# Four outputs of the next projection from un-normed sums behind four layer norms, and small VectorE steps moved in front

## The reference

```python
def layer_norm(x, g, b):
    mu = jnp.mean(x, axis=-1, keepdims=True)
    xc = x - mu
    var = jnp.mean(xc * xc, axis=-1, keepdims=True)
    return xc * lax.rsqrt(var + LN_EPS) * g + b

def swiglu(x, w_in, w_out):
    gate, up = jnp.split(x @ w_in, 2, axis=-1)
    return (jax.nn.silu(gate) * up) @ w_out
# x = LN0(a*x + swiglu(x)); x = LN1(a*x + rglru_block(x)); x = LN2(a*x + swiglu(x))
# k, v = split(x @ kv_w);   x = LN3(a*x + swiglu(x))
# x = LN4(a*x + dilated_attention(x, k, v, w_q, w_o)); x = LN5(a*x + swiglu(x))
```

## Time and profile before

| what | value |
|---|---|
| median of 3 runs | 1860.36 us (1859.71, 1860.36, 1870.26) |
| the profiled execution | 1870.4 us, its span 1868.6 us |
| TensorE busy | 98% of the span |
| VectorE, ScalarE, GpSimd busy | 68%, 62%, 22% |
| mean granted TensorE clock | 0.991 |

### The profile page before, as it was taken

How to read it: one execution, slowest core, us unless ns; L and a number is a source line. 1 busy time by engine, 2 the same in 40 slices (tenths; PEclk the granted TensorE clock), 3 DMA queues, 4 the chain that set the end, 5 groups by cost and what they waited for, 6 DMA issues and landing times.

```text
span 1868.6 us, 32954 instructions
## 1 busy us (share of the span) xinstructions
PE 1827.5 (98%) x11306; PEld 1608.9 (86%) x11306; DVE 1268.5 (68%) x1916; ACT 1165.7 (62%) x1905; POOL 418.8 (22%) x448
## 2 busy tenths in 40 slices
PE   9999999999999999999999999999999999999998
PEld 8778888898698888888889988889888888788887
DVE  7887776764776766666667866666666565667665
ACT  5476565643655746588548778744687454758853
POOL 4003320230533302021122032211021120632112
PEclk9999999999999999999999999999999999999999
DMA  7525366576353565565635546654656546026662
GB/s 247 173 69 169 114 202 191 182 194 184 108 169 102 192 189 186 177 193 189 216 116 172 186 133 194 204 179 147 187 185 203 201 130 198 35 91 201 184 220 70
DMA packets 87340, 312.11 MB, mean 167 GB/s; under 512 B 10432, under 2 KB 15680, under 8 KB 86976
## 3 DMA queue, kind: packets, MB, share of 16 engines
q1 hardware_dynamic: 86944, 309.01, 53.1%
q10 hardware_dynamic: 288, 1.64, 0.3%
HBM read 309.56 MB, written 1.05 MB: 166 GB/s over the span
## 4 chain that ended last, share of the span: by engine, by line
PE 88%; DVE 5%; ACT 3%; issue 2%; POOL 2%; DMA 0%; SPq 0%; POOLq 0%; ACTq 0%; DVEq 0%
PE pt L520 42%; PE pt L521 21%; PE pt L514 5%; PE pt L515 4%; PE pt L516 4%; PE pt L636 1%; DVE w_lo L1919 1%; PE pt L640 1%; PE pt L638 1%; PE pt L1178 1%; PE pt L959 1%; ACT w_hi L1289 1%; PE pt L1081 0%; POOL spare L2757 0%; PE pt L677 0%
## 5 line engine op out<-in xcount | busy, mean ns | idle before, releaser
L1919 DVE TENSOR_TENSOR w_lo<-raw,w_hi 128x1024 fp32r<-128x1024 f32 (+2 forms) x546 | 705.4, 1293 | 279.3 <-ACT w_hi L1289 271.2
L1289 ACT ACTIVATE w_hi<-raw 128x1024 fp32r<-128x1024 f32 (+2 forms) x546 | 597.6, 1096 | 384.3 <-PE pt L521 223.6
L520 PE MATMUL pt<-in_both,w_hi 128*128 128x512 f32 x2103 | 743.3, 398 | 0.6 <-DVE in_both L2550 0.5
L521 PE MATMUL pt<-in_both,w_lo 128*128 128x256 f32 x2103 | 590.4, 281 | 0.0
L520 PEld LDWEIGHTS pt<-in_both,w_hi 128*128 128x128 f32 x2103 | 395.6, 188 | 98.6 <-DVE w_lo L1919 1.4
L520 PE MATMUL pt<-act_both,w_hi 128*128 128x512 f32 x1309 | 463.9, 399 | 0.0
L521 PEld LDWEIGHTS pt<-in_both,w_lo 128*128 128x128 f32 x2103 | 397.8, 189 | 0.1
L521 PE MATMUL pt<-act_both,w_lo 128*128 128x256 f32 x1309 | 366.7, 280 | 0.0
L520 PEld LDWEIGHTS pt<-act_both,w_hi 128*128 128x128 f32 x1309 | 245.7, 188 | 60.8 <-issue 1.5
L521 PEld LDWEIGHTS pt<-act_both,w_lo 128*128 128x128 f32 x1309 | 247.1, 189 | 0.2
L2722 POOL TENSOR_TENSOR act_both<-scr,act_both 128x256 f32 x88 | 100.3, 1139 | 498.4 <-ACT act_both L1806 498.4
(11 more groups left out here) (341 smaller groups left out, 2337.9 us busy)
## 6 DMA issues: line engine op xcount, KB each, us to landing
raw<-in_fi SPq DMA_DIRECT2D x176, 512.0 KB, 3.6
raw<-in_ff SPq DMA_DIRECT2D x128, 512.0 KB, 3.6
raw<-in_fo SPq DMA_DIRECT2D x64, 704.0 KB, 4.1
raw<-in_dq SPq DMA_DIRECT2D x24, 512.0 KB, 3.7
raw<-in_mq SPq DMA_DIRECT2D x16, 512.0 KB, 4.0
raw<-in_mo SPq DMA_DIRECT2D x16, 512.0 KB, 3.9
raw<-in_rg_u SPq DMA_DIRECT2D x10, 512.0 KB, 3.7
raw<-in_rg_y SPq DMA_DIRECT2D x10, 512.0 KB, 3.6
```

The costliest lines, as they stand in the source:

```text
L520: nc.tensor.matmul(pt[:, b, :], lhs_hi, both.rearrange("p t s -> p (t s)"), start=start, stop=False)
L521: return nc.tensor.matmul(pt[:, b, 0:S], lhs_lo, both[:, 0, :], start=False, stop=stop)
L1289: nc.scalar.activation(w_hi[:, u.slot(), w], raw[:, u.slot(), w], ACT.Copy).then_inc(hi_split, 1)
L1919: v.tensor_tensor(w_lo[:, u.slot(), w], raw[:, u.slot(), w], w_hi[:, u.slot(), w].bitcast(F32), ALU.subtract).then_inc(lo_split, 1)
```

## The change

In front, `gains_scaled`, `softplus_begun`, `softplus_series` and `decays` move from behind `mem_k` to between the first splits of `mem_k`'s units.

Behind norms 1 to 4 (`Z_NORMS`) the next projection's first four outputs no longer wait for the norm. They are computed from z = g*y, the sums before the norm, with two more columns, the gain and the bias themselves. With W the unit's weights, the normed output is rstd * (W z - mean * W g) + W b; the last two columns of each output, W g and W b, are copied to `z_cols`. Three of the outputs run abreast and the fourth behind them, all by `three` with 258 columns. VectorE then does per output `z_open` (mean * column - output, which frees the bank) and `z_scale` (times rstd). The sums over the features become three matmuls with a full 128x128 matrix of ones (256 columns, fp32) between the second and third chunk, so mean and variance come out already spread; the root, the reciprocal (L2701, now on 128x256) and GpSimd's subtraction (all eight chunks) work on full tiles. The residual's eight ScalarE instructions move behind the splits of the next three units. Norms 0 and 5 stay as they were (`plain_norm`).

```diff
+            def from_normed_sums(name, n):
+                z = z_both(n)
+                pe.wait_ge(acc_free, LN_ACC[n] + DC - 1)
+                for k in range(DC):
+                    pe.wait_ge(z_ready, DC * (n - 1) + k + 1)
+                    for j in range(Z_OPEN):
...
+                        mm = three(o, w_hi[:, u % RING, w], w_lo[:, u % RING, w], z[:, k, 0, :], z[:, k, 1, :],
+                                   k == 0, k == DC - 1)
...
+                    if k == 1:
+                        pe.wait_ge(rest_part, REST0[n] + 3)
+                        nc.tensor.matmul(pt[:, 6, 0:S], ones, rest_sum, start=True, stop=True).then_inc(rest_ready, 1)
+                        pe.wait_ge(sq_sum, 6 * (n + 1))
+                        nc.tensor.matmul(pt[:, 4, 0:S], ones, spare[:, 0, :], start=True, stop=False)
+                        pe.wait_ge(lnsq_ready, DC * (n + 1))
+                        nc.tensor.matmul(pt[:, 4, 0:S], ones, spare[:, DC - 1, :], start=False, stop=True
+                                         ).then_inc(var_ready, 1)
+                for j in range(Z_OPEN, Z_WIDE):
...
 # ScalarE
+            def layer_norm(n):
+                z_high(n, DC - 1)
+                act.wait_ge(rest_ready, n + 1)
+                nc.scalar.activation(spread_wide, pt[:, 6, 0:S], ACT.Square, scale=1.0 / D).then_inc(rest_squared, 1)
+                nc.scalar.activation(mean_wide, pt[:, 6, 0:S], ACT.Copy, scale=1.0 / D).then_inc(rest_copied, 1)
+                act.wait_ge(var_done, n + 1)
+                nc.scalar.activation(spread_wide, spread_wide, ACT.Sqrt, bias=lneps).then_inc(ln_root, 1)
+                for k in range(DC):
+                    act.wait_ge(ln_scaled, DC * n + k + 1)
+                    shift(n, in_hi, k).then_inc(in_hi_ready, 1)
+                    if k == 5:
+                        split(Pos(LN_LAST[n] + 1 + RING))
...
 # VectorE
+            def layer_norm(n, name, first):
+                split(Pos(LN_LAST[n] + RING))
+                dve.wait_ge(var_ready, n + 1)
+                dve.wait_ge(rest_squared, n)
+                v.scalar_tensor_tensor(out=spread_wide, in0=pt[:, 4, 0:S], scalar=1.0 / D, in1=spread_wide, ...)
+                z_low(n, DC - 1)
+                dve.wait_ge(ln_root, n + 1)
+                v.reciprocal(rstd_all, spread_wide).then_inc(ln_inverse, 1)
+                for k in range(DC + 2):
+                    if k < DC:
+                        scaled(n, k)
+                    if k == DC - 1:
+                        split(Pos(LN_LAST[n] + 1 + RING))
+                        z_columns(name, 0, Z_OPEN)
+                        z_open(name, 0, first)
...
 # GpSimd
+                    for k in range(DC):
+                        pool.wait_ge(z_ready, DC * (n - 1) + k + 1)
+                        g_.tensor_tensor(y[:, k, :], y[:, k, :], mean_wide, ALU.subtract).then_inc(recentred, 1)
...
 # VectorE, in front
+            split(Pos(2))
+            gains_scaled()
+            softplus_begun()
+            split(Pos(3))
+            softplus_series((17, 15, 13, 11))
```

More of the change, by code:

```diff
@@ L121 @@
 NA_OUT_BANK = (7, 2)
+Z_SCALED0 = starts([("fi01", 2), ("kv_k", 1), ("dq", 1), ("fi11", 2)])
 LN_ACC = [ACC0[name] for name in ("fo00", "rg_out", "fo01", "fo10", "do", "fo11")]
+PLAIN = {0: 0, 5: 1}
+REST0 = [0, 2, 5, 8, 11, 14]
+RECENTRED0 = [0] + [DC - DVE_RECENTRE + DC * n for n in range(5)]
+LN_LAST = [UNIT0[name] + UNITS[name] - 1 for name in ("fo00", "rg_out", "fo01", "fo10", "do", "fo11")]
 PCOL = starts(PARAMS := [
@@ L1786, in swiglu @@
+                if held is not None:
+                    residual(n)
             def swiglu(l, f, n):
@@ L1884, in _ @@
             units("rg_out", after=ln_squares(1), hold=True)
-            layer_norm(1, UNIT0["rg_out"] + 7 + RING)
+            layer_norm(1)
             swiglu(0, 1, 2)
-            units("kv_k")
+            for j in range(1, 4):
+                split(Pos(UNIT0["kv_k"] + j + RING))
+            residual(2)
+            units("kv_k", begun=4)
             units("kv_v")
             swiglu(1, 0, 3)
-            act.wait_ge(ln_root, 4)
+            for j in range(1, Z_WIDE):
+                split(Pos(UNIT0["dq"] + j + RING))
+            act.wait_ge(z_scaled, Z_SCALED0["fi11"])
             act.dma_start(chunks(spare, 0, 8)[:, 0:3 * TRI], dram["dist"]).then_inc(dist_landed, 16)
@@ L2174, in _ @@
                 mem_low(Pos(k))
-            for u in range(2, RING):
-                split(Pos(u))
             def gains_scaled():
@@ L2540, in layer_norm @@
                 link(e)
[L2541 removed]
+                dve.wait_ge(rstd_wide, PLAIN[n] + 1)
                 for k in range(DC + 2):
@@ L2552, in layer_norm @@
                                                op0=ALU.add, op1=ALU.subtract).then_inc(in_ready, 1)
-                split(Pos(held))
+                if held is not None:
+                    split(Pos(held))
             def swiglu(l, f, n):
@@ L2651, in _ @@
             lru_lo(RC // 2 - 1)
-            units("rg_out", before=into_y_centred(1), hold=True)
-            layer_norm(1, UNIT0["rg_out"] + 7 + RING)
+            units("rg_out", before=into_y_centred(1), hold=True, ahead=z_ahead(1))
+            layer_norm(1, "fi01", act_b[0])
             swiglu(0, 1, 2)
```

296 lines of the change are left out of this document (235 added, 61 removed).

## The result

The changed kernel takes 1881.88 us (median of 4 runs, 1879.19 to 1883.01); the kernel before, run beside it, 1863.19. The ratio is 1.0087, interval 1.0067 to 1.0108: **slower by 0.9%**, some 16 us; the two medians lie 18.7 us apart. A gain of 1.5 us was forecast. The profiled execution has a span of 1877.4 us, 8.8 more than that of before.

The account below looks back on a forecast made before the run. TensorE, busy 98% of the span, bounds the kernel; 4.2 us gained in front less 2.7 lost at the norms (29.2 against 26.5) gives 1.5 us less, set against the 1860.36 median: 1859 us, range 1843 to 1871.

Parts of the forecast that it names:

- In front: Small VectorE steps moved ahead: TensorE starts in_t at 62.0 in place of 64.20, no clock fall; gain 4.2 us, range 0.5 to 5.
- The rival in which nothing comes in front: Later mem_k carries through and the clock falls anyway, so 4.2 us becomes 0.5: 1863 us; chance 0.1.
- Output 4: Fourth output behind each of norms 1 to 4 waits 2.4 us for VectorE, slowed beside GpSimd; lower bound 0.5.
- the slower rival: GpSimd's subtractions behind norms held back to 1.7 us each: 1870 us; two clock falls at unit 8 look alike, 1863; chance 0.2.
- Unit 8 of `fi01` and `fi11`: Behind norms 1 and 4 TensorE waits 3.2 us for unit 8's split, with ScalarE's residual ahead of it.
- 258 columns, the three sums: TensorE's added matmul work: three fp32 sums, 1.3 us per norm; 258 columns run as 256, under 0.1 us per norm.
- Between the last output and the sums: TensorE waits 1.6 us ahead of the sums at norms 2 and 3 only, 0.6 if GpSimd's addition does not slow.
- Behind `kv_k` and in `dq`: Behind norm 2 kv_v waits 1.8 us for VectorE's splits and key writing; behind norm 3 dq waits nothing.
- The clock: TensorE's clock falls behind waits cost 2 us each; left out of the sum and kept in the range.
- its signs of being wrong: Matmuls of 258 columns slower than 0.12 us, subtractions over 1 us, or no wait at unit 8.
- The first rival: VectorE's chain behind the norms keeps up, residual finds idle time: norms 14 us against 26.5, 16.7 less in all, 1844; chance 0.25.

Follow-up runs that it names:

- e4: Changed kernel with the reciprocal behind norms 1 to 4 written to a PSUM bank in place of SBUF; 1875.42 us, ratio 1.0041 to the kernel before.
- e6: Changed kernel with 16 unused matmuls on TensorE ahead of the wait for output 4 behind norms 1 to 4; 1882.36 us, ratio 1.0096 to the kernel before.
- e1_residual: Changed kernel with ScalarE's residual moved behind fi01 and fi11 (norms 1, 4) and ahead of the wait for dq's queries (norm 3); 1869.24 us, ratio 1.001.
- e3: Changed kernel with VectorE writing the last chunk of y ahead of three low parts of z; 1871.36 us, ratio 1.0028 to the kernel before.
- e7: Changed kernel with residual moved, last y ahead of low parts of z, and reciprocal in PSUM, all together; 1853.77 us, ratio 0.9925 to the kernel before.
- e2: Changed kernel with unit 4 split earlier on ScalarE and VectorE and output 0 opened earlier behind norms 1 to 4; 1883.44 us, ratio 1.0097.
- e8: Changed kernel with the edits of e7 plus the earlier split and opening of e2; 1857.43 us, ratio 0.9942 to the kernel before.
- f2: The kernel of e7 run once more, on the chip of the changed kernel; 1854.52 us, ratio 0.9938 to the kernel before.

## Why the prediction was wrong

It had the sum of the waits right, in part by luck, and the sign of the whole wrong. Step by step:

- **In front.** Forecast: start at 62.0, no fall, 4.2 gained. Measured: 61.88, 1.00 at 64 to 66, and -4.30 by the ninth chunk. It then lost 1.6 at 82 to 87, where the clock fell in this profile though TensorE was never idle; this happened in three of the eleven profiles with this front (this one, e4 and e6). The step held. The rival in which nothing comes in front did not.
- **Output 4.** Forecast 2.4 everywhere, by VectorE slowed beside GpSimd. Measured 2.65, 2.45, 2.65, 1.59, and e4_psum showed the reason to be the one given. GpSimd at 0.82 was in the range of the earlier trace rows; the slower rival, 1.7 us a subtraction, did not happen.
- **Unit 8 of `fi01` and `fi11`.** Forecast 3.2, by the residual. Measured 3.42 and 3.43, and e1_residual removed them.
- **258 columns, the three sums.** As counted. Products of 258 columns start 0.36 us apart as those of 256, and their matmuls are as long (296, 286 and 283 ns in the grouped view, against 288, 283 and 283). The three sums hold TensorE from 1084.18 to 1085.39, 1.2 us, where 1.3 was counted.
- **Between the last output and the sums.** Forecast a first wait at norms 2 and 3 only, 1.6 us. Measured 1.25 there, and 0.94 and 2.48 at norms 1 and 4: `y` stands behind three low parts of z on VectorE, and GpSimd's addition takes 1.57 beside the split. That I saw for norms 2 and 3 and not for 1 and 4 was a miss of 3.4 us. About half of it was made good by the first waits at norms 2 and 3, 0.7 us shorter together than forecast, and by smaller waits at units 5 to 7, 1.1 us.
- **Behind `kv_k` and in `dq`.** I had the chains the wrong way round: 1.8 for `kv_v` and nothing for `dq`. Measured: nothing (hidden behind the slow clock, 1.1 without it) and 1.80, since ScalarE, waiting for the queries of VectorE, did the residual late. The two errors, each of 1.8 us, cancel; that is luck.
- **The clock.** This is **the step that failed**: "A fall costs half of the four us behind it, 2 us each; I leave it out of the sum and in the range." The price was about right and the count was not: the term that the sum put at nothing measured 8 to 11 us over the four norms (the table below), and that alone turns the gain of 1.5 us into a loss. I argued from one idle time of two us that left the clock up and one of 4.42 that did not, and had just worked out six waits of 2.4 to 3.2 us. Five falls came, behind waits of 3.42, 2.45, 2.65, 2.48 and 3.43. The prediction did name two falls at unit 8, at 4 us, in its slower rival, but kept them out of the forecast, and its signs of being wrong have no clock in them. Nor was the idle time of two us a safe ground. It is the one ahead of norm 4, 2.17 us in the kernel before and 2.17 to 2.19 in all twelve profiles, and in three of them (e1, e3, e7) a fall followed. This is e1:

```profile
1651.78 1.22 PE L1162 MATMUL pt<-scr,con 128*128 128x256 f32 x2 [2.18 <-POOL scr L3034]
```

```profile
1652.00:1654.00 2.00, 2.00 (x8) 1.82 (x9) 0.96 (x3) 0.51 (x2) 0.00 (x0) 0.50 0.85 317
```

The price of each norm, waits and all, beside the forecast. The measured total is the excess before plus the shift by position. The matmuls are as counted in the prediction. What waits and matmuls leave of the total is put down to the falls.

| norm | before | forecast | measured | of it waits | matmuls | left | falls |
|---|---|---|---|---|---|---|---|
| 1 | 5.7 | 8.2 | 11.5 | 7.55 | 1.5 | 2.4 | 1 |
| 2 | 7.4 | 7.1 | 7.0 | 3.70 | 1.3 | 2.0 | 1 |
| 3 | 7.4 | 5.5 | 9.8 | 5.70 | 1.5 | 2.6 | 1 |
| 4 | 6.0 | 8.2 | 13.6 | 8.04 | 1.5 | 4.1 | 2 |
| sum | 26.5 | 29.0 | 41.9 | 25.0 | 5.8 | 11.1 | 5 |

Waits were 25.0 where 23.2 were forecast. By this subtraction the falls are 11.1 of the 12.9 us by which the norms are dearer than forecast, 2.2 us each; by the one fall that was there in the first profile and missing in the second, 1.6 each, they would be 8. Either way they are most of the miss at the norms. The first rival, in which VectorE keeps up and the residual finds idle time, forecast 14 us for the four norms and 1844; e7_three is that case, made: 26.5 - 9 = 17 us for the norms. It is 13.5 us under the kernel before, where the rival had 16.7.

Three things more had a part in the distance to the median. A fall in front and one in the attention, which the kernel before did not have in its profile, cost 1.6 us each. The range, 1843 to 1871, was set about a median of three runs, 1860.36; over 46 runs of the kernel before in the three later comparisons its medians were 1866 to 1867. And the profile of the changed kernel, from which the table is made, has 5 us of luck between the norms that its other executions need not have; it is the fastest of its four.

## What to carry to other kernels

When a change splits one long stop of the bounding engine into several shorter ones, count for each piece whether the clock still falls: here pieces of 2.5 us cost up to twice what they seem, and the change paid only once they were near one (e7). Before moving work off the critical place, look what it is put in front of: eight short instructions ahead of one split cost 2.6 us twice, and putting them where nothing waited for them gave these back (e1). If a repair of one wait gives nothing, see whether the next wait has grown (e2, e6). Then what is late is a chain, and handing on the wait within it gains nothing; here it helped to take work out from in front of what is waited for (e1, e3) or to make its instructions faster (e4).

## What the runs showed of the hardware

**The clock and idle time.** Behind the norms, counted over both profiles of the changed kernel and those of e1 to e8 and f2 (each wait once, a fall being windows at 0.50 directly behind it): waits of 3.2 us and more brought a fall 14 times in 15; the waits of 2.44 to 2.65 ahead of output 4, 8 times in 13; those of 2.10 to 2.49 ahead of norm 4's sums, 6 in 6; three waits of 1.80 to 1.95 for a split in `dq`, and the many up to 1.6 us, never. Elsewhere the waits do not sort the falls as well. The wait of 2.17 to 2.19 us ahead of norm 4 brought one in 3 of 12 profiles. Norm 0, which keeps its old form with many short matmuls and a wait of 1.2 us, has low stretches beside it in 7 of the 12, and the kernel before has them behind norms 2 and 3, with waits of 1.24 us. The same program, with waits that agree to 0.02 us, falls at a place in one execution and not in another. That is why a single place could not be forecast, while a sum could: by these shares the changed kernel's six waits of over two us come to 4.7 falls, and its two profiles, which are among those counted, had 5 and 4.

**Two paces of dense matmuls.** In long stretches of `halves` a pair starts every 0.3467 us, in others every 0.353, both at a granted clock of 1.00, with the same instructions. In the changed kernel the ninth pair behind 1149.88 starts at 1153.00; behind 799.74 it starts at 802.92:

```profile
1149.88 0.39 PE L550 MATMUL pt<-in_both,w_hi 128*128 128x512 f32 x1
...
1153.00 0.39 PE L550 MATMUL pt<-in_both,w_hi 128*128 128x512 f32 x1
...
799.74 0.40 PE L550 MATMUL pt<-in_both,w_hi 128*128 128x512 f32 x1
...
802.92 0.40 PE L550 MATMUL pt<-in_both,w_hi 128*128 128x512 f32 x1
```

The pace holds for a hundred pairs and more and changes at the start of a projection or behind a wait. Of the pairs of one execution, some 740 ran at the quick pace in the profile of before and some 1470 in that of the changed kernel, 4.5 to 5 us apart; in the other profiles it was 510 (e8) to some 1430 (f2). A difference of 800 such pairs, as between e7 and e8, is 5 us. This is as large as some of the effects looked for here, and it may be a part of the 10 us between two executions of one kernel. What sets it stays open: it wasn't tried.

**The VectorE and GpSimd price.** Two SBUF inputs beside GpSimd's `tensor_tensor`: 0.75 to 0.96 us for 128x256 on VectorE, where the same instructions alone start 0.39 apart, while GpSimd's eight take 6.60 in place of 6.17 us, 0.82 each in place of 0.77. With one input from PSUM (e4) the scalings take 0.42 each.
